# Products of the next unit between the pieces of a boundary, a diagonal one piece sooner and sums one part later

## What is computed

```python
x = x + rms_norm(y, post_mix_g[l])
h = rms_norm(x, pre_ffn_g[l])
x = x + rms_norm(swiglu(h, w_ffn_gate[l], w_ffn_up[l], w_ffn_down[l]), post_ffn_g[l])
```

## Time and profile before

| | |
|---|---|
| time, median of 3 runs | 1375.95 us (1375.69 to 1376.14) |
| the profiled execution's own time | 1375.85 us |
| its span, first to last instruction | 1374.0 us |
| mean granted TensorE clock | 0.998 |
| PE busy | 1350.7 us, 98% |
| DVE, ACT, POOL busy | 826.2, 533.2, 390.6 us |

### The profile page before, as it was taken

The page is one execution under the profiler, slowest core; times in us unless marked ns, Lnnn a source line. Parts: engine busy times, 40 slices in busy tenths (PEclk is TensorE's granted clock), DMA queues, the critical chain, the costliest instruction groups (busy, mean ns, idle before and its releaser), DMA issues.

```text
span 1374.0 us, 20084 instructions
## 1 busy us (share of the span) xinstructions
PE 1350.7 (98%) x8677; PEld 1270.3 (92%) x8677; DVE 826.2 (60%) x948; ACT 533.2 (39%) x752; POOL 390.6 (28%) x301
## 2 busy tenths in 40 slices
PE   8999999999999999999999999999999999999998
PEld 6999989999999999998888878998989898999997
DVE  5763676855655546567633556568676565555655
ACT  6222352442433334334344223335344342533434
POOL 3630233423324233114001111033351333323315
PEclk9999999999999999999999999999999999999999
DMA  7221122122122212142342323313222123122223
GB/s 255 99 72 62 62 111 89 63 93 91 63 92 92 92 63 93 62 162 96 109 147 63 122 94 108 139 62 138 64 91 93 62 93 93 62 93 71 85 99 130
DMA packets 89735, 131.45 MB, mean 96 GB/s; under 512 B 2656, under 2 KB 70060, under 8 KB 88879
## 3 DMA queue, kind: packets, MB, share of 16 engines
q1 hardware_dynamic: 84864, 109.16, 24.2%
q0 software_dynamic: 3808, 19.42, 3.9%
q10 hardware_dynamic: 974, 1.59, 0.4%
HBM read 114.42 MB, written 15.74 MB: 95 GB/s over the span
## 4 chain that ended last, share of the span: by engine, by line
PE 85%; DVE 9%; ACT 3%; issue 2%; POOL 1%; DMA 0%; POOLq 0%; SPq 0%; DVEq 0%; ACTq 0%
PE ps L639 26%; PE ps L630 15%; PE ps L721 11%; PE ps L676 5%; PE ps L1240 4%; PE ps L842 4%; PE ps L897 4%; PE ps L884 4%; PE ps L759 2%; PE ps L905 1%; DVE wl L1466 1%; PE ps L977 1%; DVE up L1539 1%; PE ps L776 1%; DVE up L1518 1%
## 5 line engine op out<-in xcount | busy, mean ns | idle before, releaser
L1302 DVE TENSOR_TENSOR wl<-stage,wh 128x2048 fp32r<-128x2048 f32 x53 | 131.7, 2486 | 80.7 <-ACT wh L2002 44.4
L2537 POOL TENSOR_TENSOR wsum<-stage 128x512 f32<-128x512 f32 x36 | 46.7, 1296 | 401.6 <-DVE wl L1466 249.4
L1993 ACT ACTIVATE wh<-stage 128x2048 fp32r<-128x2048 f32 x43 | 82.0, 1908 | 122.3 <-PE ps L630 69.8
L1466 DVE TENSOR_TENSOR wl<-wsum,wh 128x2048 fp32r<-128x2048 f32 x36 | 82.5, 2291 | 30.1 <-ACT wh L2022 29.8
L2095 ACT ACTIVATE gate<-ps 128x320 f32<-128x320 f32 x72 | 31.3, 434 | 142.9 <-PE ps L639 142.9
L1459 DVE TENSOR_TENSOR wbl<-stage,wbh 128x1024 fp32r<-128x1024 f32 x36 | 44.4, 1232 | 67.2 <-ACT wbh L2012 67.2
L721 PE MATMUL ps<-xh,wh 128*128 128x320 f32 x224 | 70.7, 316 | 0.2 <-DVE wl L1302 0.2
L2118 ACT ACTIVATE hh<-up 128x1280 fp32r<-128x1280 f32 x22 | 28.0, 1274 | 107.3 <-DVE up L1541 76.9
L721 PE MATMUL ps<-xh,wl 128*128 128x320 f32 x224 | 69.2, 309 | 0.0
L721 PE MATMUL ps<-xl,wh 128*128 128x320 f32 x224 | 69.2, 309 | 0.0
L2448 POOL TENSOR_TENSOR small<-small 64x5 f32<-64x5 f32 (+1 forms) x10 | 12.2, 1222 | 196.0 <-DVE small L1320 196.0
(11 more groups left out here) (391 smaller groups left out, 4513.9 us busy)
## 6 DMA issues: line engine op xcount, KB each, us to landing
stage<-w_ffn_gate SPq DMA_DIRECT2D x22, 1024.0 KB, 5.3
stage<-w_ffn_up SPq DMA_DIRECT2D x22, 1024.0 KB, 5.3
stage<-w_ffn_down SPq DMA_DIRECT2D x22, 1024.0 KB, 5.0
stage<-w_in_odd SPq DMA_DIRECT2D x12, 1024.0 KB, 5.2
x_spill<-x POOLq DMA_DIRECT2D x3, 2560.0 KB, 10.2
x<-x_spill SPq DMA_DIRECT2D x3, 2560.0 KB, 10.2
stage<-w_in_even SPq DMA_DIRECT2D x5, 1024.0 KB, 7.0
stage<-w_out_even SPq DMA_DIRECT2D x4, 1024.0 KB, 5.3
```

What stands on the lines that cost most here:

```text
L1302: dve.tensor_tensor(wl[:, s].rearrange("p k c -> p (k c)"), stage[:, s, :], f32(wh[:, s].rearrange("p k c -> p (k c)")), ALU.subtract).the ...
L1466: dve.tensor_tensor(wsl[:, u % 2, :], wsum[:].rearrange("p i c -> p (i c)"), f32(wsh[:, u % 2, :]), ALU.subtract).then_inc(w_lo, 1)
L1993: act.activation(wsh[:, u % 2, :], flat_stage(u), ACT.Copy).then_inc(w_hi, 1)
```

## The change

Three things are moved; no arithmetic is added or left out.

1. Of the next unit's 48 matmuls for its first column block, the 16 for half 0 with high weights are issued among the pieces of half 1: two before piece 8 and one ahead of each wait for `xh` or `xl` from there on, until they are used up at piece 14. The other 16 with high weights, for half 1, follow the pieces, then the 16 with low weights.
2. VectorE makes the diagonal of the second half at piece 6, not 7.
3. PE's sums of x's squares no longer stand directly behind those 48 matmuls: PE first waits for the weights of the part that follows and does three blocks (9 matmuls) of it, then the sums. In the first and third boundary the spread moves from between the two halves of the second column block to behind three blocks of the second half. In the second boundary the sums are moved likewise into the first part of the following unit, and its spread stays between its column blocks.

```diff
@@ boundary, block.tensor
-                out = banks4(g)
+                out, next_out, v = banks4(g), banks4(g + 1), u + 1
                 pe.wait_ge(w_lo, u + 1)
                 pe.wait_ge(acc_empty, g - 1)
+                def next_first(k, n, h):
+                    w, mv_ = ((wh, xh), (wh, xl), (wl, xh))[n]
+                    return pe.matmul(next_out[:, 0, h, :], w[:, v % 2, k, 0:P], mv_[:, k, h * HALF:(h + 1) * HALF],
+                                     start=(k == 0 and n == 0), stop=(k == KB - 1 and n == 2))
+                ahead_of_wait = [(k, n) for k in range(KB) for n in range(2)]
                 for i in range(PIECES):
                     h, k = divmod(i, KB)
+                    if i == KB:
+                        wait_ahead(pe, B, ahead_hi, w_hi)
+                        for _ in range(2):
+                            next_first(*ahead_of_wait.pop(0), 0)
                     for n, (w, mv_, ready) in enumerate(((wh, xh, xh_done), (wl, xh, None), (wh, xl, xl_done))):
                         if ready is not None:
+                            if h == 1 and ahead_of_wait:
+                                next_first(*ahead_of_wait.pop(0), 0)
                             pe.wait_ge(ready, B["x"] + i + 1)
...
-                out, v = banks4(g + 1), u + 1
-                wait_ahead(pe, B, ahead_hi, w_hi)
-                def first(passes):
...
-                first(((0, (wh, xh)), (1, (wh, xl))))
+                for n in range(2):
+                    for k in range(KB):
+                        next_first(k, n, 1)
                 wait_ahead(pe, B, ahead_lo, w_lo)
-                last = first(((2, (wl, xh)),))
+                for k in range(KB):
+                    for h in range(2):
+                        last = next_first(k, 2, h)
+                def x_sums():
+                    pe.wait_ge(x_squares_added, 4 * (B["n"] + 1))
+                    sum_tiles(bank, acc[:, 0], range(TT), first=True).then_inc(sums_full, 1)
                 if blocks == 1:
                     last.then_inc(w_used, 1)
-                pe.wait_ge(x_squares_added, 4 * (B["n"] + 1))
-                sum_tiles(bank, acc[:, 0], range(TT), first=True).then_inc(sums_full, 1)
-                if blocks == 1:
+                    pe.wait_ge(w_lo, U_QKS[1] + 1)
+                    pe.wait_ge(acc_empty, G_QKS[1] - 1)
+                    wv, out = views(U_QKS[1]), banks4(G_QKS[1])
+                    part(wv, out, xh, xl, 0, 0, range(3), KB)
+                    x_sums()
+                    part(wv, out, xh, xl, 0, 0, range(3, KB), KB)
+                    part(wv, out, xh, xl, 0, 1, range(KB), KB)
                     return
-                if blocks == 2:
-                    pe.wait_ge(w_lo, u + 2)
-                    part(views(v), out, xh, xl, 1, 0, range(KB), KB)
-                    pe.wait_ge(acc_empty, g + 1)
-                    spread(pre_norm(B["n"]), first_banks(B))
-                    pe.wait_ge(ms_done, pre_norm(B["n"]) + 1)
-                    part(views(v), out, xh, xl, 1, 1, range(KB), KB).then_inc(w_used, 1)
-                    pe.wait_ge(rs_done, 2 + B["n"])
-                    return
-                spread(pre_norm(B["n"]), ahead)
+                pe.wait_ge(w_lo, u + 2)
+                part(views(v), next_out, xh, xl, 1, 0, range(3), KB)
+                x_sums()
+                part(views(v), next_out, xh, xl, 1, 0, range(3, KB), KB)
+                pe.wait_ge(ms_done, pre_norm(B["n"]) + 1)
+                part(views(v), next_out, xh, xl, 1, 1, range(3), KB)
+                pe.wait_ge(acc_empty, g + 1)
+                spread(pre_norm(B["n"]), first_banks(B))
+                part(views(v), next_out, xh, xl, 1, 1, range(3, KB), KB).then_inc(w_used, 1)
                 pe.wait_ge(rs_done, 2 + B["n"])
@@ behind boundary(BOUNDS[1], U_QK, blocks=1)
-            pe.wait_ge(w_lo, U_QKS[1] + 1)
-            pe.wait_ge(acc_empty, G_QKS[1] - 1)
-            for m in range(2):
-                if m == 1:
-                    spread(pre_norm(1), norm_banks(G_QK)[2])
-                for h in range(2):
-                    last = part(views(U_QKS[1]), banks4(G_QKS[1]), xh, xl, m, h, range(KB), KB)
+            spread(pre_norm(1), norm_banks(G_QK)[2])
+            for h in range(2):
+                last = part(views(U_QKS[1]), banks4(G_QKS[1]), xh, xl, 1, h, range(KB), KB)
@@ boundary, block.vector
-                    elif i == 7:
+                    elif i == 6:
                         half_diag(B, 1)
```

More of the change, by code:

```diff
@@ L766, in boundary @@
                 last.then_inc(w_used, 1)
-                out, v = banks4(g + 1), u + 1
-                wait_ahead(pe, B, ahead_hi, w_hi)
-                def first(passes):
-                    for n, (w, mv_) in passes:
-                        for k in range(KB):
-                            wt = w[:, v % 2, k, 0:P]
-                            for h in range(2):
-                                last = pe.matmul(out[:, 0, h, :], wt, mv_[:, k, h * HALF:(h + 1) * HALF],
-                                                 start=(k == 0 and n == 0), stop=(k == KB - 1 and n == 2))
-                    return last
```

## The result

The changed kernel takes **1386.32 us** (median of 4, 1383.64 to 1387.18) against 1376.05 (1375.69 to 1376.24): a ratio of 1.0069 (95% interval 1.0057 to 1.0082). It is slower by 10 us, ten times the forecast, and 7 us beyond the range. The profiled execution has a span of 1384.8, 10.8 more than the 1374.0 of before; its mean granted clock is 0.992 instead of 0.998.

A forecast was written before the change was run, and what follows sets the result against it. TensorE, busy 98% of the span, bounds the kernel. The gain goes to the wait for w_lo: 0.09 + 0.84 + 0.09 = 1.0 us slower, 1375.95 + 1.0 = 1376.9 us; range 1375.2 to 1379.2.

The forecast's parts named there:

- The products: Pieces 8 to 15: 16 products moved in make TensorE run without gaps; by itself 1.7 us gained a boundary.
- The diagonal: VectorE's second-half diagonal, a piece sooner: 0.48 us instead of 1.16, so the spread comes 0.3 us sooner.
- The wait: TensorE behind the low-weight products: stands for w_lo 2.0 us in boundaries one and three, 3.05 in the second.
- The sum without the clock: Three boundaries at full clock: 0.09, 0.84 and 0.09 us slower, 1.0 in all.
- From there it has what stood behind 194.84 before: First boundary after the w_lo wait: sums, 48 products and a spread take 9.23 us, plus 0.11 for a first product.
- the fall of the clock: Rival: TensorE's clock falls in the new waits; second boundary alone 1378.4 us, chance 0.17; all three 1381.3, chance 0.05.
- needs a wait of about 2.5 us: Clock rival's condition, from the kernel's end: clock fell to 0.50 2.5 us after the last matmul.
- the others' 2.0 are shorter: First and third boundaries: waits of 2.0 us against the second's 3.05, where the clock can fall.
- in all three: Rival case: the clock falls in every boundary, 5.35 us slower in all, 1381.3 us; chance 0.05.
- 1.05 to 1.85 a fall: Price of one clock fall in a boundary: half of the 2.1 to 3.7 us at the low clock.
- the 2.1 to 3.7: Time in us at the low clock per fall, read from slow 512-column matmuls at the kernel's start.
- my sum: The three boundaries' forecast slowdown at full clock, 0.09 + 0.84 + 0.09 = 1.0 us.

The follow-up runs named there:

- e11: Changed kernel with low weights sooner, sums later and no waits, but the 16 products back behind the pieces: 1375.56 us, ratio 0.9995.
- e10: Changed kernel with low weights sooner, sums later and no waits, but the diagonal back at piece 7: 1371.14 us, ratio 0.9965.
- e3: Changed kernel with 12 unread matmuls (20 in the second boundary) filling each wait for w_lo: 1377.87 us, ratio 1.0019.
- e7: Changed kernel with the sums behind all 8 blocks and the spread behind 6 blocks of the second half, waits kept: 1380.12 us, ratio 1.003.
- e6: Kernel before with part 3 of the change only (sums behind the wait and three blocks, spread later): 1379.0 us, ratio 1.0022.
- e2: Kernel before with part 1 of the change only (the 16 products among the pieces): 1377.61 us, ratio 1.0013.
- e9: Changed kernel again, unchanged, timed and traced later: 1386.3 us, ratio 1.0072.
- e1: Kernel before with only the second half's diagonal moved to piece 6 from 7: 1376.27 us, ratio 1.0003.

## Why the prediction was wrong

**The products, right.** The pieces ended 20.52 us after their start; 188.16 meant 20.24. The gain was confirmed by e11.

**The diagonal, right in kind.** 0.47 at piece 6, late by `xl` of piece 5: TensorE waits 0.17 for it and spreads thereafter, as written. 0.2 instead of 0.3 us. What the trace of before could not tell is that 1.16 is one outcome of two; the Trainium skill (SBUF — State Buffer, section "SBUF: two separate sides") has it that whoever starts first keeps the shared pair for its whole instruction. e10's two pairs of lengths agree that one holds up the other (1.15 with 1.11, 0.47 with 1.50), but not on which: the add's record begins 0.30 us ahead in both, and in the second it was the add that took longer.

**The wait, right.** From the first piece, TensorE was to reach the wait after 24.93 us and to leave it after 26.90; it left after 27.01, having stood for 1.81 us, and 2.89 and 1.81 in the others (2.0, 3.05 and 2.0 were forecast). The sum without the clock, 0.09 + 0.84 + 0.09, measured 0.19 + 0.92 + 0.22 = 1.33 in e3.

**What failed** is the step "From there it has what stood behind 194.84 before", priced at 9.23 us, and behind it the rival that should have broken it. Those 9.23 + 0.11 took 207.45 - 196.58 = 10.87; in e3, with the wait filled, they took 204.41 - 195.08 = 9.33. I had put the fall of the clock down as a rival that "needs a wait of about 2.5 us" and set "the others' 2.0 are shorter" against it. That bound came from one place, the end of the kernel, where nothing ran after the wait, so it showed the delay of a fall and not what is enough for one. The runs put three things in its place. The condition: a wait of 1.81 came before a fall with the sums far off (e7), and waits of 1.81 (changed kernel), 1.20 (e6) and even 0.68 (e2) did when the sums, ten matmuls of one column in 1.03 us, stood close by. I had moved those sums close behind the wait and priced them at 1.03 us of dense work; with them farther off the kernel loses 6 us less (e7), though not all of that can be put down to them. The chance: "in all three" had 0.05, and it happened in both traces of the changed kernel (and the mean clock of all its eight runs was 0.991 to 0.994). The size: 1.05 to 1.85 a fall; measured 1.54 (1.73 - 0.19), 3.15 and 3.12, since two of three spells last 6.8 us, longer than the 2.1 to 3.7 read off the kernel's start. That reading was weak besides: the profile gives the granted clock of 8 to 11 us as 1.00, so its matmuls of 0.63 us don't show a low clock by the column that I went by elsewhere.

The account of the 10.8 us in the profiled execution: 1.33 my sum, 7.81 the clock, 1.65 ahead of the first boundary.

**What stays open.** The 1.65 lie in code that the change doesn't touch. Over all thirteen traces the first piece starts between 167.87 (e7) and 169.68 (e9); the one of before, 167.92, is at the low end, and e7, which has all three parts of the change, is lower still. Part of it is seen at the kernel's very start, in a window of TensorE of the changed kernel:

```profile
11.00:14.00 3.00, 3.00 (x13) 1.00 1.02 383
```

The kernel before and e7 do 16 matmuls in that window, e1 11, e9 12, all of the same two lines of code: it varies between kernels whose code is equal up to there. No run here shows it to come from the change, and none excludes a part of it. What exactly the chip asks for before it lowers the clock was not found either: e7's 2.88 us passed and its 1.81 did not, and the changed kernel's 2.89 fell after the same work as e7's 2.88. The order of the work alone does not settle it, and no run here varied anything else by itself.

## What to carry to other kernels

Before moving work ahead of a wait, find out whether the producer of what is waited for moves too; here VectorE's order had to change with TensorE's, and then the change gained 4 us instead of losing 10. On an engine that is busy for 98%, price a new wait not by its length alone but also by the granted clock behind it, and treat matmuls of few columns close behind it as part of the risk: they stood there in most of the falls seen here. Read the clock in windows behind a wait, in more than one execution, for the loss stands in busy time and not in any list of waits.

## What the runs showed that I had not expected

- The granted clock mostly falls when the wait is over: 0.6 us after it in e7 and 0.9 to 2.6 us after it in the changed kernel, with TensorE at work again. It then stayed at 0.50 for 3.4 or 6.8 us in every such spell of a boundary.
- Waits as short as 0.57 and 0.68 us, directly before ten matmuls of one column, came before a fall (e2), while 2.88 us with dense work on both sides did not (e7), although the changed kernel fell after the same wait and the same work.
- VectorE's diagonal and GpSimd's add, where they overlap, come out as one of two stable pairs of lengths, 1.15 and 1.11 or 0.47 and 1.50, from records that begin 0.30 us apart in the same order (e10); a duration read from one trace can be the worse or the better of the two.
- Run again, the changed kernel fell within 0.3 us of the same places, for the same lengths (e9).
